# Feed-forward stages in seven half-size products: Strassen pairs of up tiles with down tiles between them

## The reference, cut to what matters

```python
# x is [1, 512, 1024] float32; every stage: x = x + stage(x)
def _rmsnorm(x, g):
    y = x * lax.rsqrt(jnp.mean(x * x, axis=-1, keepdims=True) + RMS_EPS)
    return y * g

def _mlp(x, norm_g, w1, w2):                 # w1 [1024, 4096], w2 [4096, 1024]
    h = _rmsnorm(x, norm_g)
    return jnp.square(jax.nn.relu(h @ w1)) @ w2

x = x + mixed @ w_out;        x = x + mlp(x, norm2_g, w_ff_up, w_ff_down)          # layer 1
x = x + _even_mixer(x, ...);  x = x + _mlp(x, mlp_norm[0], w_mlp_in[0], w_mlp_out[0])
x = x + _odd_mixer(x, ...);   x = x + _mlp(x, mlp_norm[1], w_mlp_in[1], w_mlp_out[1])
```

## Time and profile before

| | us |
|---|---|
| median of 3 runs | 2378.03 |
| lowest, highest | 2377.58, 2381.52 |
| span of the profiled execution | 2376.0 |
| busy: PE, PEld, DVE, ACT, POOL | 2350.2, 1918.1, 1330.4, 936.5, 156.3 |

### The profile page before, as it was taken

How to read it: one execution, slowest core, us unless ns; L and a number is a source line. 1 busy time by engine, 2 the same in 40 slices (tenths; PEclk the granted TensorE clock), 3 DMA queues, 4 the chain that set the end, 5 groups by cost and what they waited for, 6 DMA issues and landing times.

```text
span 2376.0 us, 32832 instructions
## 1 busy us (share of the span) xinstructions
PE 2350.2 (99%) x12976; PEld 1918.1 (81%) x12976; DVE 1330.4 (56%) x1963; ACT 936.5 (39%) x1475; POOL 156.3 (7%) x196
## 2 busy tenths in 40 slices
PE   8999999999999999999999999999999999999999
PEld 6877778787888888877678888888888888888887
DVE  7656556778553443567764334356755557533433
ACT  5444464457242332446553223243423224422321
POOL 5111110000002200012220000000000000000000
PEclk9999999999999999999999999999999999999999
DMA  4222223222333323321033233322222212333322
GB/s 161 71 72 69 66 61 109 73 71 81 98 96 111 104 88 96 106 62 54 27 98 106 89 98 106 88 89 89 77 66 81 88 57 80 120 89 99 99 88 78
DMA packets 60639, 205.80 MB, mean 87 GB/s; under 512 B 7249, under 2 KB 7249, under 8 KB 60386
## 3 DMA queue, kind: packets, MB, share of 16 engines
q1 hardware_dynamic: 59760, 202.93, 28.5%
q10 hardware_dynamic: 754, 1.14, 0.2%
HBM read 201.94 MB, written 2.10 MB: 86 GB/s over the span
## 4 chain that ended last, share of the span: by engine, by line
PE 94%; DVE 3%; ACT 1%; issue 1%; POOL 1%; DMA 0%; SPq 0%; DVEq 0%; ACTq 0%
PE psum L1724 84%; PE psum L1785 1%; PE psum L1887 1%; PE psum L1751 1%; PE psum L1858 1%; PE psum L1792 1%; PE psum L1840 1%; PE psum L1881 1%; POOL arena L597 1%; PE psum L1802 0%; PE psum L1798 0%; PE psum L1760 0%; PE psum L1830 0%; DVE arena L1325 0%; DVE cols L1331 0%
## 5 line engine op out<-in xcount | busy, mean ns | idle before, releaser
L1724 PE MATMUL psum<-hhi,whi 128*128 128x512 f32 x1640 | 646.3, 394 | 10.4 <-DVE wlo L1048 8.4
L1724 PE MATMUL psum<-hlo,whi 128*128 128x512 f32 x1640 | 643.9, 393 | 0.0
L1724 PE MATMUL psum<-hhi,wlo 128*128 128x512 f32 x1640 | 642.0, 391 | 0.0
L1724 PE MATMUL psum<-uhi,whi 128*128 128x512 f32 x1392 | 545.7, 392 | 0.0
L1724 PE MATMUL psum<-ulo,whi 128*128 128x512 f32 x1392 | 544.1, 391 | 0.0
L1724 PE MATMUL psum<-uhi,wlo 128*128 128x512 f32 x1392 | 542.9, 390 | 0.0
L1048 DVE TENSOR_TENSOR wlo<-raw,whi 128x1024 fp32r<-128x1024 f32 (+1 forms) x399 | 466.8, 1170 | 57.0 <-ACT whi L1010 31.6
L1724 PEld LDWEIGHTS psum<-hhi,whi 128*128 128x128 f32 x1640 | 308.4, 188 | 76.1 <-issue 12.1
L1724 PEld LDWEIGHTS psum<-hhi,wlo 128*128 128x128 f32 x1640 | 308.4, 188 | 64.3 <-issue 0.2
L1724 PEld LDWEIGHTS psum<-hlo,whi 128*128 128x128 f32 x1640 | 308.7, 188 | 61.7 <-issue 0.2
L1010 ACT CAST whi<-raw 128x1024 fp32r<-128x1024 f32 x190 | 199.6, 1051 | 351.9 <-PE psum L1724 351.9
(11 more groups left out here) (251 smaller groups left out, 1758.4 us busy)
## 6 DMA issues: line engine op xcount, KB each, us to landing
raw<-in_packed_dram SPq DMA_DIRECT2D x359, 512.0 KB, 3.6
raw<-in_packed_dram SPq DMA_DIRECT2D x40, 256.0 KB, 2.6
x<-in_xt_dram SPq DMA_DIRECT2D x8, 256.0 KB, 5.5
out_dram<-x SPq DMA_DIRECT2D x8, 256.0 KB, 2.0
arena<-in_near_bias_dram ACTq DMA_DIRECT2D x1, 1024.0 KB, 6.1
vec<-in_vec_dram ACTq DMA_DIRECT2D x1, 44.0 KB, 4.1
arena<-in_gla_gate_up_dram ACTq DMA_DIRECT2D x1, 32.0 KB
arena<-in_gla_gate_bias_dram ACTq DMA_DIRECT2D x1, 2.0 KB
```

What stands on the lines that cost most here:

```text
L1724: mm = pe.matmul(g, w[:, u % 4, k, :], v[:, k, :], start=n == 0, stop=n == 3 * kt - 1)
```

## The change

The four blocks of a stage become one run of 64 units: six plain up tiles, two down tiles, then 13 times (a pair of up units, two down units), and four down units.

- A pair of up units computes two output tiles together. Weights and activations are cut in two by two blocks (512 input features by 128 output features; 512 input features by 256 tokens), and Winograd's form of Strassen's scheme makes the result from 7 block products in place of 8. A block product (`block_product`) is 4 tiles times 3 matmuls of 256 columns: 84 matmuls in a pair.
- POOL makes the sums of weight blocks from `raw` (`weight_sums`, four sums of 512 columns per pair, one of them in place), ACT and DVE split three of them (`diff_high`, `diff_low`, 1536 columns); the fourth sits in `raw` and is split with its unit.
- The activation sums are made once a stage, while the plain up tiles run: ACT scales (`h_scale`), DVE subtracts (`h_sum`), ACT casts (`sums_high`), DVE makes the low part (`sums_low`), four rounds of it.
- The products are added on DVE (`first_sums`, `last_sums`) with one copy on ACT (`copy_product`), then squared, cast and split for two tiles at once.
- A down unit (`fall`) has half of the input features (512) of a 1024-wide block and two output tiles; its 24 matmuls have 512 columns as before. `x` gets 1024 columns at a time.
- The new tiles `blocks`, `diffs` and `parts` lie over `arena`. So the load of `near_bias` and the masks on POOL wait until the last pair of the first stage is through. The loops are gone; the program is written out.

```diff
--- before.py
+++ after.py
+PLAIN = 6
...
     def ff(i, w1, w2, row):
         steps[f"ff{i}"] = len(units)
-        for f in range(FB):
-            for j in range(KD):
-                units.append(("up", w1, row, f * D + P * j, KD, j))
-            for j in range(KD):
-                units.append(("down", w2, row * 4 + f * D, P * j, KD, j))
+        def fall(e):
+            units.append(("fall", w2, row * 4 + 512 * (e // 4), 256 * (e % 4), KD, e))
+        for j in range(PLAIN):
+            units.append(("up", w1, row, P * j, KD, j))
+        for e in range(2):
+            fall(e)
+        for p in range(PLAIN // 2, 16):
+            for half in range(2):
+                units.append(("upper", w1, row, 256 * p, KD, (p, half)))
+            for e in range(2):
+                fall(2 * (p - PLAIN // 2) + 2 + e)
+        for e in range(28, 32):
+            fall(e)
...
-        arena = sb("arena", [P, 17000])
+        with nc.sbuf_tensor("arena", [P, 17000], F32) as arena:
+            pass
+        blocks = sb("blocks", [P, 2, KD, SEQ], F32R)
+        diffs = sb("diffs", [P, 2, 12, P], F32R)
+        parts = sb("parts", [P, 17000 - 8192 - 3072])
...
+            def weight_sums(q):
+                u = pair_unit(q)
+                v = u + 1
+                for w in (u, v):
+                    pool.wait_ge(raw_in[w % 4], 16 * (w // 4 + 1))
+                if q:
+                    pool.wait_ge(diff_lo_done, q)
...
+                pool.tensor_tensor(s3, a11, a21, ALU.subtract).then_inc(w_sums, 1)
+                pool.wait_ge(w_sums, 4 * q + 1)
+                pool.tensor_tensor(a21, a21, a22, ALU.add).then_inc(w_sums, 1)
+                pool.wait_ge(w_sums, 4 * q + 2)
+                pool.tensor_tensor(s2, a21, a11, ALU.subtract).then_inc(w_sums, 1)
+                pool.wait_ge(w_sums, 4 * q + 3)
+                pool.tensor_tensor(s4, a12, s2, ALU.subtract).then_inc(w_sums, 1)
...
-            pool.wait_ge(norm_lo, KD * (ORDER["ff0"] + 1))
+            stage_sums(0)
+            pool.wait_ge(posted, last_up(0) + 1)
...
+            def h_scale(n, j):
...
+                if j:
+                    act.wait_ge(h_sums, 3 * (4 * i + j))
+                for a in range(2):
+                    k = 2 * j + a
+                    nc.scalar.activation(h_parts[:, 2 * a:2 * a + 2, :], x[:, k, :].rearrange("p (b t) -> p b t", b=2), ACT.Copy,
+                                         scale=gain(name, k0 + k)).then_inc(h_scaled, 1)
+            def sums_high(n, j):
+                i = FFNORMS.index(n)
+                act.wait_ge(h_sums, 3 * (4 * i + j) + 3)
+                nc.scalar.copy(sums_hi[:, j, :, :], h_parts[:, 4:8, :]).then_inc(sums_hi_done, 1)
+            def diff_high(q):
+                act.wait_ge(w_sums, 4 * q + 4)
+                if q:
+                    act.wait_ge(product, 7 * q)
+                nc.scalar.copy(diff_hi, w_diff).then_inc(diff_hi_done, 1)
+            def copy_product(q):
+                act.wait_ge(product, 7 * q + 4)
+                if q:
+                    act.wait_ge(up_added, 4 * q - 3)
+                nc.scalar.copy(up_mid[:, 2, :], psum[:, 2, 0:HALF_T]).then_inc(up_copied, 1)
+            def finish_pair(u):
...
+                act.wait_ge(up_scaled, q + 1)
+                nc.scalar.activation(up_out, up_out, ACT.Square).then_inc(act_step, 1)
+                act.wait_ge(act_step, chain.up())
+                o = first_operand[0][:, rows_of(p), :]
+                nc.scalar.copy(o, up_out.rearrange("p (a b) t -> p a (b t)", a=2)).then_inc(up_high, 1)
             def ff(i):
                 b, n = steps[f"ff{i}"], ORDER[f"ff{i}"]
-                ff_block(b, 0, n)
-                if i == 0:
-                    act.wait_ge(norm_lo, KD * (n + 1))
-                    act.dma_start(sinks, a["sink_a_2"].partition_broadcast(P)).then_inc(sink_in, 16)
-                    act.dma_start(near_bias, a["near_bias"].rearrange("p (h k) -> p h k", h=HEADS)).then_inc(rpb_in, 16)
...
+                following = n + 1
+                for j in range(PLAIN + 2):
+                    split_hi(b + j + 2)
+                    if j == 0:
+                        norm(n)
+                    if 1 <= j <= PLAIN:
+                        continue_with(b + j - 1)
+                    if 1 <= j <= 4:
+                        h_scale(n, j - 1)
+                    if 2 <= j <= 5:
+                        sums_high(n, j - 2)
+                q = STAGE_PAIRS * i
+                diff_high(q)
+                split_hi(b + PLAIN + 4)
+                for v in range(b + PLAIN + 2, b + 60, 4):
+                    split_hi(v + 3)
+                    split_hi(v + 4)
+                    copy_product(pair_of(v))
+                    split_hi(v + 5)
+                    if v < b + 56:
+                        diff_high(pair_of(v) + 1)
+                    finish_pair(v)
+                    split_hi(v + 6)
...
+                    if m == 0 and i == 0:
+                        act.wait_ge(posted, last_up(0) + 1)
+                        act.dma_start(sinks, a["sink_a_2"].partition_broadcast(P)).then_inc(sink_in, 16)
+                        act.dma_start(near_bias, a["near_bias"].rearrange("p (h k) -> p h k", h=HEADS)).then_inc(rpb_in, 16)
...
+            def h_sum(n, j):
+                i = FFNORMS.index(n)
+                c = 3 * (4 * i + j)
+                dve.wait_ge(h_scaled, 2 * (4 * i + j) + 2)
+                if j:
+                    dve.wait_ge(sums_lo_done, 4 * i + j)
+                dve.tensor_tensor(h_parts[:, 4:6, :], h_parts[:, 1:4:2, :], h_parts[:, 0:2, :], ALU.subtract).then_inc(h_sums, 1)
+                dve.wait_ge(h_sums, c + 1)
+                dve.tensor_tensor(h_parts[:, 6, :], h_parts[:, 3, :], h_parts[:, 4, :], ALU.subtract).then_inc(h_sums, 1)
+                dve.wait_ge(h_sums, c + 2)
+                dve.tensor_tensor(h_parts[:, 7, :], h_parts[:, 2, :], h_parts[:, 6, :], ALU.subtract).then_inc(h_sums, 1)
+            def sums_low(n, j):
+                i = FFNORMS.index(n)
+                dve.wait_ge(sums_hi_done, 4 * i + j + 1)
+                dve.tensor_tensor(sums_lo[:, j, :, :], h_parts[:, 4:8, :], sums_hi[:, j, :, :].bitcast(F32),
+                                  ALU.subtract).then_inc(sums_lo_done, 1)
+            def diff_low(q):
+                dve.wait_ge(diff_hi_done, q + 1)
+                dve.tensor_tensor(diff_lo, w_diff, diff_hi.bitcast(F32), ALU.subtract).then_inc(diff_lo_done, 1)
...
+            def first_sums(q):
+                dve.wait_ge(product, 7 * q + 5)
+                if q:
+                    dve.wait_ge(posted, pair_unit(q - 1) + 2)
+                dve.wait_ge(up_copied, q + 1)
+                dve.tensor_tensor(up_out[:, 0:2, :], twice(up_mid[:, 2, :]), bank_pair(0), ALU.add).then_inc(up_added, 1)
+            def last_sums(q):
+                dve.wait_ge(product, 7 * q + 7)
+                dve.wait_ge(up_added, 4 * q + 1)
+                dve.tensor_tensor(up_mid[:, 0:2, :], twice(up_out[:, 1, :]), bank_pair(3), ALU.add).then_inc(up_added, 1)
+                dve.wait_ge(up_added, 4 * q + 2)
+                dve.tensor_tensor(up_out[:, 1, :], up_mid[:, 0, :], psum[:, 1, HALF_T:SEQ], ALU.add).then_inc(up_added, 1)
+                dve.tensor_tensor(up_out[:, 2:4, :], twice(up_mid[:, 1, :]), bank_pair(1), ALU.add).then_inc(up_added, 1)
+                dve.wait_ge(up_added, 4 * q + 4)
...
+            def post_pair(u):
...
+                dve.wait_ge(up_high, q + 1)
+                dve.tensor_tensor(lo, up_out.rearrange("p (a b) t -> p a (b t)", a=2), hi.bitcast(F32),
+                                  ALU.subtract).then_inc(posted, 2)
...
+            def ff(i):
+                b, n = steps[f"ff{i}"], ORDER[f"ff{i}"]
+                following = n + 1
+                q = STAGE_PAIRS * i
+                for j in range(PLAIN + 2):
+                    if j == 1:
                         norm_low(n)
                         dve.wait_ge(norm_rstd, n + 1)
...
+                    if 1 <= j <= PLAIN:
+                        evacuate(b + j - 1)
+                    split_lo(b + j + 2)
+                    if 1 <= j <= PLAIN:
+                        post(b + j - 1)
+                    if 3 <= j <= 6:
+                        sums_low(n, j - 3)
+                    if 2 <= j <= 5:
+                        h_sum(n, j - 2)
+                diff_low(q)
+                post_fall(b + PLAIN)
+                split_lo(b + PLAIN + 4)
+                for v in range(b + PLAIN + 2, b + 60, 4):
+                    q = pair_of(v)
+                    post_fall(v - 1)
+                    split_lo(v + 3)
+                    split_lo(v + 4)
+                    first_sums(q)
+                    split_lo(v + 5)
+                    last_sums(q)
+                    if v < b + 56:
+                        diff_low(q + 1)
+                    post_pair(v)
+                    post_fall(v + 2)
+                    split_lo(v + 6)
...
```

(37 more changed lines are left out.)

278 lines of the change are left out of this document (178 added, 100 removed).

## The result

The changed kernel takes 2360.86 us (median of 4 runs, 2359.30 to 2363.25) against 2377.86 (2377.58 to 2381.52) on the same chip: 0.9926 of the time, 95% interval 0.9912 to 0.9940. The forecast was 2338.0: the gain is 17.0 us where 40 were expected. The time lies outside the forecast's own bounds (2325 to 2356) and inside the range that the rivals widened; the nearest value on record is the rival at 2356.

The account below looks back on a forecast made before the run. PE's matmul number and distance were taken to bound the feed-forward stages. Gain 53.0 less 10.8 (stage starts) and 2 (masks) gave 40.2 us off 2376.0: span 2335.8, median 2338; bounds 2325 to 2356, widened by rivals to 2317 to 2364.

Parts of the forecast that it names:

- the forecast's own bounds: Whole kernel: 2325 to 2356 us, from a start loss of 0 to 8 a stage and masks of 0 to 6.
- the rival at 2356: Pairs' matmuls: the fp32r extra belongs to each instruction, distance 0.119 us, net gain 21.7 us; chance 0.22.
- 39 pairs: Feed-forward up units: a pair takes 9.52 us instead of 10.88, gaining 1.36 each, 53.0 us in all.
- start of a stage: Before a stage's first block product: PE waits 3.6 us for the activation sums, costing 10.8 us over three stages.
- masks, window stage: After the first feed-forward stage: POOL's later masks may hold up DVE; 2 us lost, ends 0 and 6.
- Both say 0.113: Pairs' block products: both neighbouring readings put the distance of 256-column fp32r matmuls at 0.113 us; 0.1134 taken.
- The two witnesses: Matmul distance at 256 columns: half of 512 fp32r columns, 0.1134 us, and the retention's 128-column float32 instructions, 0.1125.
- The rival that gave the extra to the instruction: Pairs' matmuls: fp32r's extra 0.011 us over float32 is per instruction, not per column; 0.119, kernel 2356, chance 0.22.
- The forecast's own sign of being wrong: Pairs: wrong if the distance at 256 columns is 0.12 us or more, or PE waits in mid-stage.
- The rival at 2582: Pairs' matmuls: weight loads do not fit behind 256 columns, so matmuls follow at 0.188 us; 204 us slower, chance 0.07.
- Plain tiles and down units: Feed-forward stages: 18 plain up tiles and 96 down units have the matmuls they had; no gain or loss.
- The pair's loop: Steady loop of pairs: DVE needs 14.6 us of a 20.4 us period, smallest cover 5 us, nothing lost.

Follow-up runs that it names:

- the kernel with the sums first: Changed kernel with DVE's sums_low and h_sum ahead of the weight split and post at a stage's start: 2347.20 us, 0.9869.
- the tile 64 bytes further on: Changed kernel with 64 more bytes per partition ahead of arena, so blocks, diffs and parts start 64 bytes later: 2367.42 us, 0.9951.
- the two window selects moved ahead: Changed kernel with POOL's two selects for the window bias ahead of its last 16 selects for near_bias: 2361.45 us, 0.9926.
- at 112 bytes: Changed kernel with the pairs' moving operands 112 bytes behind the weights modulo 128: 2366.38 us, 0.9949; with DVE's activation sums first too: 2351.78, 0.9891.
- everything 64 bytes apart: Changed kernel with activation sums and diffs 64 bytes higher: 2370.18 us, 0.9964; with DVE's activation sums first too: 2352.19, 0.9888.

## Why the prediction came out half right

The spans in us saved, step by step (stages by windows, the pair 9.88, the kernel with the sums first as the measure of the wait):

| step | forecast | measured |
|---|---|---|
| 39 pairs | +53.0 | +39.0 (39 x 1.00) |
| plain up tiles | 0 | -2.9 (3 x 144 x 6.6 ns) |
| down units | 0 | -1.8 (2304 matmuls, 227.5 for 226.7) |
| start of a stage | -10.8 | -10.95 |
| clock at half after it | none | -1.6 |
| masks, window stage | -2 | -2.85 |
| other stages | 0 | -0.7 (ahead of the first stage -0.9, retention +0.2) |
| sum | 40.2 | 18.2 (spans: 18.1) |

- **The step that failed** is "Both say 0.113": the distance of 256-column matmuls is 0.1176 in the mean, not 0.1134, and that is 14 of the 22 us. The two witnesses agreed by accident. Half of 512 columns shares out an extra that, at equal addresses, belongs to each instruction (0.0133). The other witness, the 128-column float32 instructions of the earlier trace rows, says nothing of what a column costs if it stood at the floor of 112 ns that fp32r has for anything up to about 240 columns. No run tried float32, but the single starts of those sixteen lie 111.7 ns apart, the floor's own value (111.7 at 128, 192 and 224 columns of fp32r). The rival that gave the extra to the instruction had the mechanism for equal addresses; its 0.119 lies 1 ns from the 120.0 measured there. The forecast's own sign of being wrong, 0.12 or more, was set too high: at 0.1176 a quarter of the pairs' gain was already gone. Part of the products is faster than 120 only because `blocks` and `diffs` lie 64 bytes off.
- **The floor**: a load of 188 ns does not bound matmuls 113 to 120 ns apart (PEld is busy 9.87 of 9.88 us in a pair, and loads overlap one another). The rival at 2582 fell; these runs also don't bear out the rule of the Trainium skill (TensorE: Matmul & The Clock Gate, The mechanism) that a load overlaps a matmul only when its row group differs: these all use all rows. The same page's N / 2.4 + 2.5 ns (Back-to-back issue gap), an estimated 109.2 at 256 columns, is 4 to 11 ns under what the seven products take. What makes the floor at 112 ns was not isolated; a load's pace is the natural suspect, only argued.
- **Plain tiles and down units** were put at nothing on the ground that they have the matmuls they had. They have other operands: moving `blocks` costs 6.6 ns a matmul by its address, shown by the tile 64 bytes further on. Where the 0.8 ns of the down units come from stays open.
- **The start of a stage** was right in place and cause, and in size by some luck: PE was ready at 44.95 us (forecast 44.0) and the sums at 48.6 (forecast 47.6), and the two misses cancel. That a wait of 3 us can be followed by 3.4 us at half clock was not in the sum. It came in one of the three stages of this trace, in all three with the tile 64 bytes on, with the two window selects moved ahead, and at 112 bytes, in two of three with everything 64 bytes apart and with the masks left out, and in none of the four kernels in which the wait was gone.
- **The masks**: DVE waited 2.02 us, forecast 0 to 3, and the stage lost 2.85, forecast 2. The sum had only the wait; it lacked the 1.1 us by which the selects slow DVE down while they run beside it.
- **The pair's loop** has room, as forecast: DVE works 14.7 us, by its groups, in a period of 20.8 (forecast 14.6), and PE has no wait in it.

Not settled: why one set of addresses has two paces, and which rule of the addresses holds; whether a layout exists in which the whole pair runs at 113; and what makes the clock fall in the window stage. It fell there in the traces of seven of the ten kernels with pairs, also with the masks left out and PE's waits those of the kernel before.

## What to carry to other kernels

Take the price of a smaller instruction from a line through two sizes, not from one size halved: here N / 2.4 + 13.3 ns at equal addresses, with a floor of 112. Two neighbours that agree prove little if one of them may stand at a floor. A scheme that trades columns for instructions pays the fixed part each time: 84 of 256 for 48 of 512 saves 12.5% of the columns and 7.4 to 9.2% of the time. And when work is put ahead of a deadline on an engine that keeps its order, put the link of the longest chain first; that was worth about 12.5 us here, nearly as much as the misjudged distance.

## What the runs showed of the hardware

- The pace of fp32r matmuls depends on where the operands lie in SBUF: 113.3 to 130.0 ns at 256 columns, 226.7 to 233.3 at 512, with nothing else running. Of the addresses tried, 512 columns are fastest (226.7) where weights and moving operand lie equal, and 256 are not (120.0 there, 113.3 at best).
- In 14 of the 18 waits of 3 us before a first block product (six traces) PE's granted clock fell to half for 3.4 us, beginning between 0.4 us before and 1.4 us after the work began again; it cost 1.4 to 1.7 us each time.
- DVE's instructions can be slower while POOL runs selects: copies of 64x512 float32 took 0.72 and 0.74 us beside them and 0.42 without.
